# Expert rows of the first token tile: 28 of 128 taken from TensorE, scaled on ScalarE and added on GpSimd

## What is computed

```python
q = (hc @ w_query).reshape(PEER_CHUNK, PEER_HEADS, PEER_KEY_DIM)
...
gate = jax.nn.softmax(top_s.astype(jnp.float32), axis=-1).astype(hc.dtype)
u = jnp.take(expert_u, experts, axis=0)
act = jax.nn.gelu(jnp.einsum('chkd,cd->chk', u, hc))
v = jnp.take(expert_v, experts, axis=0)
return jnp.einsum('chk,chkd->cd', gate * act, v)
```

## Time and profile before

| | before |
|---|---|
| three runs, us | 2481.38, 2481.76, 2489.49 |
| profiled execution, span from its first to its last instruction, us | 2484.5 |
| TensorE busy, us (share) | 2227.9 (90%) |
| VectorE busy | 1689.0 (68%) |
| ScalarE busy | 718.1 (29%) |
| GpSimd busy | 632.5 (25%) |
| read from HBM | 746.39 MB, 301 GB/s over the span |

### The profile page before, as it was taken

The page is one execution under the profiler, slowest core; times in us unless marked ns, Lnnn a source line. Parts: engine busy times, 40 slices in busy tenths (PEclk is TensorE's granted clock), DMA queues, the critical chain, the costliest instruction groups (busy, mean ns, idle before and its releaser), DMA issues.

```text
span 2484.5 us, 25065 instructions
## 1 busy us (share of the span) xinstructions
PE 2227.9 (90%) x8150; PEld 1439.7 (58%) x8150; DVE 1689.0 (68%) x3748; ACT 718.1 (29%) x2019; POOL 632.5 (25%) x606
## 2 busy tenths in 40 slices
PE   6999998989999998999998899899898977777776
PEld 3444876648887886777775666575444433333232
DVE  5553754636655945897988999777667666676654
ACT  2321122421101112332323233224334333333332
POOL 2100000000010001332334343334444344344332
PEclk8999997999999999999999999999999999999999
DMA  9531002127685445999999999999999999999997
GB/s 353 193 108 54 26 1 68 52 72 237 226 295 194 145 143 212 408 405 383 386 396 411 410 402 383 374 393 420 420 420 421 422 421 421 421 415 422 421 417 304
DMA packets 130627, 749.95 MB, mean 302 GB/s; under 512 B 14416, under 2 KB 14544, under 8 KB 64464
## 3 DMA queue, kind: packets, MB, share of 16 engines
q0 software_dynamic: 87456, 588.90, 58.7%
q1 hardware_dynamic: 43056, 159.65, 18.0%
HBM read 746.39 MB, written 2.10 MB: 301 GB/s over the span
## 4 chain that ended last, share of the span: by engine, by line
PE 55%; DMA 26%; DVE 12%; ACT 4%; issue 2%; another core or an unknown queue 0%; POOL 0%; DVEq 0%; SPq 0%; ACTq 0%; POOLq 0%
PE PS L580 55%; DMA arena<-experts_dram,ecur 22%; DVE arena L2339 4%; DVE h_all L1652 2%; DMA ring<-up_dram 1%; DVE arena L1646 1%; DMA ring<-down_dram 1%; ACT const L1534 1%; ACT L1526 1%; ACT arena L1530 1%; DVE arena L1652 1%; DMA ring<-branch_dram 1%; DVE h_all L1646 1%; DVE arena L1973 0%; DMA xT<-x_dram 0%
## 5 line engine op out<-in xcount | busy, mean ns | idle before, releaser
L580 PE MATMUL PS<-arena,const 128*128 128x512 f32 (+2 forms) x1772 | 838.1, 618 | 175.7 <-ACT const L1534 168.1
L580 PE MATMUL PS<-h_all,ring 128*128 128x256 f32 (+2 forms) x3584 | 888.9, 406 | 20.2 <-ACT h_all L1202 7.7
L2510 POOL DMA_INDIRECT arena<-experts_dram,ecur x512 | 583.4, 1139 | 1109.9 <-PE PS L580 718.6
L2339 DVE CUSTOM_DVE_ANT_0 arena<-arena 128x1024 f32<-128x1024 f32 x512 | 625.9, 1222 | 291.7 <-DMA arena<-experts_dram,ecur 287.7
L580 PEld LDWEIGHTS PS<-h_all,ring 128*128 128x128 f32 x3584 | 683.1, 192 | 235.1 <-issue 141.8
L580 PEld LDWEIGHTS PS<-arena,const 128*128 128x128 f32 (+1 forms) x1772 | 336.3, 196 | 602.3 <-issue 341.9
L1526 ACT ACTIVATE arena<-arena 128x2 f32<-128x2 f32 x255 | 51.6, 202 | 717.7 <-DVE arena L2339 717.3
L580 PE MATMUL PS<-arena,ring 128*128 128x256 f32 (+1 forms) x960 | 238.9, 408 | 3.8 <-DMA ring<-down_dram 3.0
L580 PEld LDWEIGHTS PS<-arena,ring 128*128 128x128 f32 x960 | 181.6, 190 | 61.1 <-issue 33.7
L580 PE MATMUL PS<-arena 128*128 128x128 f32 (+3 forms) x1104 | 160.1, 303 | 13.7 <-ACT arena L1337 6.5
L580 PEld LDWEIGHTS PS<-arena 128*128 128x128 f32 (+1 forms) x1104 | 140.3, 200 | 38.8 <-issue 13.8
(11 more groups left out here) (254 smaller groups left out, 1438.5 us busy)
## 6 DMA issues: line engine op xcount, KB each, us to landing
ring<-up_dram SPq DMA_DIRECT2D x88, 512.0 KB, 3.4
ring<-w_in_dram SPq DMA_DIRECT2D x80, 512.0 KB, 4.1
arena<-ada_dram POOLq DMA_DIRECT2D x80, 512.0 KB, 5.4
ring<-query_dram SPq DMA_DIRECT2D x32, 512.0 KB
ring<-w_out_dram SPq DMA_DIRECT2D x24, 512.0 KB, 3.9
ring<-down_dram SPq DMA_DIRECT2D x16, 704.0 KB, 6.0
ring<-branch_dram SPq DMA_DIRECT2D x16, 512.0 KB
arena<-experts_dram,ecur POOLq DMA_INDIRECT x512
```

The lines of the kernel that those rows point to most:

```text
L580: return nc.tensor.matmul(o, l, r, start=start, stop=stop)
L2339: V.tensor_tensor_reduce(out=u, in0=u, in1=hrow[:, (r // HEADS) % 2, :], scale=1.0, scalar=0.0, op0=MUL, op1=ADD, accum_out=dots[:, p % NB ...
L2510: nc.gpsimd.indirect_dma_start(out=ring_e[:, g % RING, :], out_offset=None, in_=a["experts"], in_offset=bass.IndirectOffsetOnAxis(ap=ecur[ ...
```

## The change

28 rows of the first tile, the even rows of pairs 1, 3, ... 47 (24 rows) and of pairs 53, 55, 57 and 59 (4 rows), are no longer multiplied on TensorE. ScalarE multiplies v by its weight in place, in the ring (128x1024), instead of writing the diagonal. GpSimd copies the first of these rows into `prow` and adds the others to it. The operation on row g stands in GpSimd's queue right behind the issue of the gather of row g+6. Slots of these rows are released by GpSimd's count `pool_used`. Ahead of the tile's last pair TensorE waits for all 28 and adds `prow` to PSUM with two matmuls by the identity. In pairs 1 to 47 TensorE then keeps the even rows of pairs 2, 6, ... 46, 12 rows; the rows of pair 0 and of pairs 48 to 63 that are in neither list stay with it too.

```diff
+POOLED = [2 * p for p in (*range(1, 48, 2), *range(53, 60, 2))]
+POOL_LAG = 6
...
+def pooled(g):
+    return sum(q < g for q in POOLED)
...
 def by_tensor(g):
-    return g - sides(g)
+    return g - sides(g) - pooled(g)
...
 def tensor_rows(p):
-    return [k for k in range(BATCH) if BATCH * p + k not in SIDE]
+    return [k for k in range(BATCH) if BATCH * p + k not in SIDE and BATCH * p + k not in POOLED]
...
                 pe.wait_ge(side_used, sides(BATCH * TILE * (c + 1)))
                 for v in range(2):
                     mm(PS[:, v, :], ident, side[:, v * S:(v + 1) * S], False, False)
+                if c == 0:
+                    pe.wait_ge(pool_used, pooled(BATCH * TILE))
+                    for v in range(2):
+                        mm(PS[:, v, :], ident, prow[:, v * S:(v + 1) * S], False, False)
...
-                if old >= 0 and len(tensor_rows(old)) < BATCH:
+                if old >= 0 and any(BATCH * old + k in SIDE for k in range(BATCH)):
                     act.wait_ge(side_used, sides(BATCH * (old + 1)))
-                if old >= 0 and BATCH * (old + 1) in SIDE:
+                if old >= 0 and (BATCH * (old + 1) in SIDE or BATCH * (old + 1) in POOLED):
                     act.wait_ge(rows_used, by_tensor(BATCH * (old + 1)))
...
+                for k in range(BATCH):
+                    if BATCH * p + k in POOLED:
+                        act.wait_ge(w_ready2, BATCH * p + k + 1)
+                        row = ring_e[:, (BATCH * p + k) % RING, D:]
+                        A(row, row, ACT.Copy, scale=wts[:, b, k:k + 1]).then_inc(row_scaled, 1)
                 rows = tensor_rows(p)
...
+            def pool_row(g):
+                row = ring_e[:, g % RING, D:]
+                pool.wait_ge(row_scaled, pooled(g + 1))
+                if g == POOLED[0]:
+                    nc.gpsimd.tensor_copy(prow, row).then_inc(pool_used, 1)
+                else:
+                    pool.wait_ge(pool_used, pooled(g))
+                    nc.gpsimd.tensor_tensor(out=prow, in0=row, in1=prow, op=ALU.add).then_inc(pool_used, 1)
...
                     if old >= 0 and old in SIDE:
                         pool.wait_ge(side_used, sides(old + 1))
+                    elif old >= 0 and old in POOLED:
+                        pool.wait_ge(pool_used, pooled(old + 1))
                     elif old >= 0:
                         pool.wait_ge(rows_used, by_tensor(old + 1))
                     nc.gpsimd.indirect_dma_start(
...
                     ).then_inc(row_landed[g % RING], 16)
+                    if g - POOL_LAG in POOLED:
+                        pool_row(g - POOL_LAG)
```

More of the change, by code:

```diff
@@ L373, in build @@
         side_used = sem("side_used")
+        pool_used = sem("pool_used")
+        row_scaled = sem("row_scaled")
         blocks_done = sem("blocks_done")
```

## The result

The changed kernel takes 2495.64 us (median of ten runs, 2490.22 to 2500.94), the kernel before 2481.24 us (median of ten, 2477.12 to 2489.49). The ratio is 1.0051, 95% interval 1.0038 to 1.0064: 9 to 16 us slower, where 6 us faster was forecast. The profiled execution took 2497.28 us and has a span of 2495.6 us.

A forecast was written before the change was run, and what follows sets the result against it. First tile: TensorE, DMA close behind; later tiles: DMA. With pairs 1 to 47 then bound by bytes (335 us) and VectorE (333), plus 2, 337 replaced 345 (-8); +1.7 gave about -6: 2476 us, range 2464 to 2500.

The forecast's parts named there:

- What bounds the kernel: First tile bound by TensorE with DMA close behind, later tiles by DMA alone; TensorE busy 335.7 of 345 us.
- what is taken from TensorE: Rows at 1.71 us each: 41 us off TensorE in pairs 1 to 47, 7 us in pairs 53 to 59.
- the weights take over a part: In pairs 1 to 47, 76 blocks need 312 us for weight loads, 332 if a load takes 9.5 us.
- The bytes: Pairs 1 to 47 must move 136.89 MB: 335 us at 409 GB/s, 10 less than now.
- GpSimd's add and its queue: Adds of 2.25 us, 54 us in pairs 1 to 47, lie within GpSimd's 236.9 us of idle time.
- ScalarE: Scaling passes of 1.06 us replace diagonals of 0.387: 19 us more, 16 in pairs 1 to 47, costed at nothing.
- The margin in the queue: At pair 9, GpSimd's add would end 0.5 us before the next gather can begin; more behind row 28.
- VectorE beside GpSimd: In pairs 1 to 47 VectorE loses 27 us, half of the adds' 54, making its limit 333 us.
- The end of the tile and pairs 53 to 59: Two more matmuls at the tile's end cost 1.7 us; the 7 us off TensorE in these pairs bring nothing.
- The third case, VectorE and GpSimd shut out: Every one of 24 adds in pairs 1 to 47 blocks VectorE: 360 us there, 2499 us in all; chance 0.22.
- the rule that it cites: A VectorE instruction with two SBUF inputs and a GpSimd instruction reading SBUF exclude each other; up to 54 us lost.
- its forecast: Whole kernel at 2476 us, about 6 us faster; the case from 2470 to 2483 us had chance 0.45.

The follow-up runs named there:

- adds only: Kernel before, TensorE keeping all its rows, with 27 adds of the same size put into GpSimd's queue, their sum unused: 2496.5 us, ratio 1.0068.
- the three experiments whose GpSimd doesn't: Changed kernel with adds left out (2473.1 us) or replaced with writing zeros (2469.5 us); kernel before with the 28 rows put on VectorE (2494.7 us).
- the run with eight chosen rows: Changed kernel with only the even rows of pairs 6, 11, 15, 19, 27, 29, 33 and 37 moved off TensorE: 2478.2 us, ratio 0.9989.

## Why the prediction was wrong, step by step

**What bounds the kernel; what is taken from TensorE.** Right, but for a reading of the slices: of the last fifteen, TensorE stands at 7 or 6 in the last eight alone; in the seven ahead of them it stands at 8 or 9, and five of these move 420 GB/s or more. Nothing in the sum hangs on it. 56 records of 128x512 are left, and in the run without adds TensorE stands 10.2 us before its `up` loads, where it had stood 2.7: the weights take over a part, as was said, but not all.

**The bytes.** Right. Without adds the stretch took 332 us at 412 GB/s, where 335 at 409 were worked out. That 41 us of matmuls are worth about 10 was the best step of the prediction.

**GpSimd's add and its queue; ScalarE.** Right. An add takes 2.36 us where 2.25 were taken, and waits 5.2 us in 22 of them for its row. ScalarE's pass takes 1.13 us, not 1.06, and hides. The margin in the queue is narrow, as was said: with the adds two rows earlier it is gone.

**VectorE beside GpSimd.** This is the step that failed, in two ways. First the size: it took half of the 54 us, 27, because two-operand passes fill about half of VectorE's time, as if adds fell at random. They don't. 24 of the 27 adds follow a gather whose slot a side row of VectorE had just let go, and four waited for ScalarE's scaling behind a pair's dots; so an add begins at about the moment of the next dot, and 26 of 27 held something. In pairs 1 to 47 the dots alone lost 144.3 - 114.6 = 30 us, the casts 4: 34 in place of 27. Second the idle time: 292.8 + 27 + half of the other 27 idle us gave a limit of 333 us, beside the bytes' 335. Measured, VectorE is busy for 326.0 us and idle for 21.1 of the 347.1 of its stretch, where 13 had been left to it. The term was 7 us short in what is held and 8 in what stays idle, and VectorE's stretch was not 333 but 347 us, above the bytes. The two runs that frame it: with TensorE at its old load, 43 us held cost 15 (adds only); with TensorE relieved, from no adds (-8) to the changed kernel (+14), 37 us held cost 22, VectorE being then the busiest engine.

**The end of the tile and pairs 53 to 59.** Costed at +1.7 and nothing. The two matmuls more show in no run: with them, and without adds in pairs 53 to 59, the dots from row 106 to row 128 take 74.8 to 76.2 us, and 75.9 before. The prediction named GpSimd's queue and the backlog of gathers as the cover; what has little cover there is VectorE, which in the kernel before was busy for 54.0 of the 62 us from 1358 on the earlier trace rows and for 25 of the last 26:

```profile
1410.00:1436.00 26.00, 23.12 (x77) 14.95 (x76) 25.00 (x53) 6.22 (x21) 10.69 (x9) 0.93 0.98 398
```

The adds of these four rows hold its dots for 5 us, and a cast and a tensor-tensor operation for 2 and 2.5 more. In the two profiles the dots fall back by another 4.8 us between row 106 and row 128 (3.1 to 7.9 us late).

**The rivals.** The third case, VectorE and GpSimd shut out, gave 2499 us and a point of decision at 37 us held; 2495.6 us were measured with some 34 in the stretch. Its mechanism is shown: longer dots in every kernel whose GpSimd reads at these places, none longer than 1.30 us in the three experiments whose GpSimd doesn't (but for the copy of the first row in two of them). That its time came so near is in part luck: it had 360 us for pairs 1 to 47, where the profile has 347, and nothing for pairs 53 to 59, which cost about 4. It had 0.22. The reason given against it (VectorE stands idle for 52 us, where an add can hide) was the mistake: an add that begins just ahead of a dot doesn't hide in idle time elsewhere. The prediction itself called this case the likelier by the rule that it cites, and yet gave it less than half the chance of its forecast.

**What stays open.** The profiles differ by 11.1 us and the medians by 14.4. The prediction took the 2.7 us by which the span of before exceeds the median as something that carries over; in the changed kernel the span is 1.7 us under the time of its own execution, so the profile of before is, by the same 1.7, one of an execution of some 2486 us, slower than its median. Of the 11.1 us the profiles place 1.8 in pairs 1 to 47, 4.8 in pairs 53 to 64, some 3 behind row 192, where nothing was changed, and 1.3 ahead of the tile. The 3 us (from row 192 to 224, 97.2 us where it took 93.7) are in no other run with adds (92.7 to 94.7) and stay unexplained. Nor is 1.8 us the price of the 24 rows: in the run with these rows alone the same stretch took 352 us and not 347. The profiles of these kernels differ by up to 12 us in where the first dot of pair 1 stands, before any change can act, so a single pair of profiles doesn't divide 14 us; the medians carry the verdict. A kernel that beats the one before and still adds up all its rows was not shown: the run with eight chosen rows has an interval that ends at 1.0003.

## What to carry to other kernels

An idle GpSimd isn't free help for a busy VectorE: price each GpSimd operation that reads on-chip memory at up to its full length on VectorE wherever VectorE makes passes with two operands (here 1.4 of 2.4 us on average, in dots alone), and ask at which instant the operation is released, not how much idle time the engines have on average. Here a row cost VectorE 1.4 us by way of GpSimd and 1.28 us done by itself. Before moving work off the bound, work out what comes next (here the bytes, at 10 of 41 us): the prize was small, and a loss of some 47 us on the second engine, dots and all, was enough to turn it.

## What the runs showed of the hardware that was not expected

- A dot can be held although it began first. Timelines of the changed kernel:

```profile
1173.70 3.73 DVE L2359 CUSTOM_DVE_ANT_0 arena<-arena 128x1024 f32<-128x1024 f32 x1
...
1173.97 2.37 POOL L2529 TENSOR_TENSOR arena<-arena 128x1024 f32<-128x1024 f32 x1
...
1236.11 2.86 POOL L2529 TENSOR_TENSOR arena<-arena 128x1024 f32<-128x1024 f32 x1 [2.27 <-ACT arena L1550]
```

  The dot at 1173.70 is recorded 0.27 us before the add, and ends 1.1 us after it. The add at 1236.11 began 0.57 us behind a dot, which took its usual 1.22 us, and is itself 0.5 us longer: there the dot kept it waiting. The page SBUF — State Buffer of the Trainium skill (section SBUF: two separate sides) says that whichever starts first gets the shared ports for its whole instruction. By the recorded starts this trace doesn't agree: in the changed kernel five dots recorded up to 0.51 us ahead of an add were held, and six recorded 0.57 us or more ahead ran on. With the adds 4 rows behind, a dot recorded only 0.15 us ahead ran on, beside an add of 3.28 us. One reading is that some tenths of a microsecond of a record lie ahead of the engine's first read; no run shows it directly.
- A cast of 128x32 numbers, 0.177 us otherwise, took 2.32 us when it came beside an add (two of the 6 casts of this kind, 5.3 us, in pairs 1 to 47): a tiny instruction with one operand is held as long as a large one.
- In the changed kernel VectorE's passes with an operand in PSUM were never longer beside an add: 33 of them, none by more than 0.001 us.
- Cutting GpSimd's operation in four let VectorE in between pieces only in part: beside 10 of the 28 rows a dot waited for the fourth piece (3.21 us for the one shown), and the kernel was no faster.
